# Splitting the weight tiles of an encoder trunk in pairs instead of one by one

## The chip, the cores and the metric

One Trainium2 chip, one NeuronCore. The metric is the time of one execution in device microseconds (us); the median of the runs is compared. Engines: TensorE (PE) multiplies, VectorE (DVE) and ScalarE (ACT) work elementwise, GpSimd (POOL) helps, SyncE (SP) issues the DMAs.

## The reference

A two-layer encoder trunk over 256 tokens of width 2048, float32. Cut to the matrix products that carry the weights:

```python
def reference(x, mem, ...):
    mem_n = rmsnorm(mem, mem_norm_g)
    h = x
    for layer in range(2):
        xn = rmsnorm(h, tok_norm_g[layer])
        if layer == 0:   # gated DeltaNet, two directions, 12 heads of 128, chunks of 64
            mix, q_mem = deltanet_mixer(xn, dn_w_in[0], dn_conv_w[0], ...)
        else:            # gMLP: gelu(u) * (w_s @ rmsnorm(gelu(v)) + b_s), chunks of 128 tokens
            mix, q_mem = spatial_gating_mixer(xn, gm_w_in[0], gm_v_norm_g[0], gm_w_s[0], gm_b_s[0])
        mo = memory_attention(q_mem, mem_n, mem_w_kv[layer])      # 4 heads, 256 memory tokens
        h = h + jnp.concatenate([mix, mo], axis=-1) @ tok_w_out[layer]
        hn = rmsnorm(h, ffn_norm_g[layer])
        h = h + jnp.square(jax.nn.relu(hn @ ffn_w1[layer])) @ ffn_w2[layer]   # hidden 8192
    return rmsnorm(h, final_norm_g)
```

## The kernel before, in words

All weights (some 400 MB) are read once, in tiles of 128 rows by 512 columns, 256 KB. A block is 16 such tiles, that is one strip of 512 columns over 2048 rows; two neighbouring tiles are a slab, so a block has 8 slabs. There are 96 blocks, 1536 tiles. A product in float32 is made from three products with rounded operands: every tile is split into `w_hi`, its rounded value, and `w_lo`, the rest, and the activations (`xT_hi`, `xT_lo`, or `hid_hi`, `hid_lo`) likewise.

Four engines pass each tile on:

- SyncE (`load`, L343) transfers tile kt of block B to `raw[:, kt % 8]`. There are 8 slots; a slot is free again when TensorE has used the tile that was in it (`tile_used`).
- ScalarE (`split`, L981) waits until the tile has landed and copies it, rounded, to `w_hi`; it counts up `hi_ready`.
- VectorE (`split`, L1451) waits for that and subtracts: `w_lo = raw - w_hi`. `w_lo` lies on the same bytes as `raw`. It counts up `tiles_split`.
- TensorE waits for `tiles_split` and multiplies. In `slab` (L467) a tile takes 6 matmuls: for each of two groups of 128 tokens hi x hi, hi x lo, lo x hi (L479, L480, L481). In `up_slab` (L485, the first product of the FFN, whose result is wanted transposed) the tile is the stationary operand and takes 8 matmuls: 4 pieces of 128 columns by 2 (L498, L500).

The order of the work is written out by hand. ScalarE and VectorE split two slabs ahead of TensorE: their loops call `split((t + 2) // 8, (t + 2) % 8)` at step t, and the FFN does the same with `head(B)` (slabs 0 and 1 of a block) and `tail(B)` (slabs 2 to 7). Between the splits stand the other pieces of each engine's work, in program order: `beside(stages, steps)` (L322) takes one stage of the side work after each slab. In the DeltaNet part (blocks 3 to 20) such a stage is a piece of the convolution (`convolve`, L1644, L1657), of the normalisation, of the triangular solve by levels (L1741 on), and so on; GpSimd makes the decay operands (L2104, L2107), two masks (L2128, L2130) and a scaling (L2132) there. In the FFN ScalarE drains a block's result (`up_highs`, L1328), VectorE adds and applies relu (`relu_result`, L1900, L1910), GpSimd squares it (`square_hidden`, L2146), and ScalarE and VectorE split it (`hidden`, L1336 and L1927). At the end of a down block VectorE adds the result to `h` (`add_result`, L1922).

An engine works in program order, so an instruction that waits holds all that stands behind it on its engine.

Of the kernel before, what the change touches and what calls it, by code (L numbers as in the profile page):

```python
# [8 lines left out]
F32 = mybir.dt.float32  # L9
F32R = mybir.dt.float32r  # L10
ACT = mybir.ActivationFunctionType
ALU = mybir.AluOpType
# [115 lines left out]
def encoder_trunk(nc, x, mem, mem_columns, consts, mem_norm_g, tok_norm_g, dn_w_in, dn_conv_w, dn_a_log, dn_dt_bias,  # L128
# [5 lines left out]
    def sem(name):  # L134
        if name not in sem_of:
            sem_of[name] = ctx.enter_context(nc.semaphore(name))
        return sem_of[name]
# [4 lines left out]
    with ctx:  # L142
# [126 lines left out]
        hi_ready = sem("hi_ready")  # L269
        tiles_split = sem("tiles_split")  # L270
        tile_used = sem("tile_used")
# [194 lines left out]
        def _(pe):  # L466
            def slab(B, s, R, parity, kt0, act_hi, act_lo, first, last):  # L467

                for k in range(2):
                    kt = kt0 + k  # L470
                    slot = (2 * s + k) % SLOTS
                    pe.wait_ge(tiles_split, B * 16 + (2 * s + k + 1))
                    start = first and k == 0
# [11 lines left out]
            def up_slab(B, s, R, parity, j, odd=None):  # L485

                for k in range(2):
                    kt = 2 * s + k
                    slot = kt % SLOTS
                    pe.wait_ge(tiles_split, B * 16 + (kt + 1))  # L490
                    for f in range(4):
# [374 lines left out]
            def ffn(layer, next_steps, next_fill=None):  # L866


                for half in range(2):
# [15 lines left out]
                    def last_down(early=3):  # L885
# [5 lines left out]
                        for m in range(2):  # L891
                            tokens = slice(m * P, (m + 1) * P)
                            acc = banks[2 * ((R_FFN[layer] + 11) % 2) + m][:]
                            for kt in range(KT - 2 * early, KT):
                                if m == 0:
                                    pe.wait_ge(tiles_split, B * 16 + kt + 1)
                                slot, ht = kt % SLOTS, KT + kt
# [82 lines left out]
        def _(act):  # L980
            def split(B, s):  # L981

                for kt in (2 * s, 2 * s + 1):
                    slot = kt % SLOTS
                    act.wait_ge(landed[slot], B * 32 + 16 * (kt // SLOTS + 1))
                    act.activation(w_hi[:, slot], raw[:, slot], ACT.Copy).then_inc(hi_ready, 1)  # L986

# [455 lines left out]
        def _(dve):  # L1443
# [7 lines left out]
            def split(B, s):  # L1451

                for kt in (2 * s, 2 * s + 1):
                    slot = kt % SLOTS
                    dve.wait_ge(hi_ready, B * 16 + (kt + 1))
                    dve.tensor_tensor(w_lo[:, slot], raw[:, slot], w_hi[:, slot].bitcast(F32), ALU.subtract  # L1456
                                      ).then_inc(tiles_split, 1)

# [729 lines left out]
```

## Time and profile before

| | us |
|---|---|
| median of 3 runs | 2420.52 |
| lowest and highest run | 2420.32, 2421.28 |
| span of the profiled execution | 2423.1 |
| TensorE, busy in it | 2364.7 |
| VectorE, busy in it | 1557.7 |
| ScalarE, busy in it | 1245.0 |
| GpSimd, busy in it | 169.1 |

The runs agree within 1 us. The span is that of one execution under the profiler, from its first to its last instruction; the page gives no other time of that execution. Busy time of an engine is the time in which at least one of its instructions runs. Matmuls overlap: one of 512 columns is shown as some 390 ns long, but they start 227 ns apart, so a busy TensorE is not one at its peak. The profile names a group by its line in the kernel, its engine, and what it writes and reads; idle time "before" a group is put down to what ended it.

### The profile page before, as it was taken

To read this page: it belongs to the slowest core of one execution; us is meant where nothing else is said; L and a number is where in the kernel's file an instruction comes from. 1 tells how busy PE (TensorE), PEld (TensorE's weight loads), DVE (VectorE), ACT (ScalarE), POOL (GpSimd) and SP (SyncE) were. 2 spreads that over 40 slices of the span, in tenths; PEclk is the share of its full clock that TensorE was granted. 3 is DMA by queue.
4 is the path that set the end of the run, shared out by engine and by line. 5 is a ranking of instruction groups with operands and counts; after the bars stand their busy time and mean duration, and the time that the engine had idled before them with its cause. 6 is when DMAs were issued, how large, how long until landed. Compare 5 with 4: busy or idle time off the path is not lost.

```text
span 2423.1 us, 37472 instructions
## 1 busy us (share of the span) xinstructions
PE 2364.7 (98%) x12069; PEld 2002.1 (83%) x12069; DVE 1557.7 (64%) x2481; ACT 1245.0 (51%) x2205; POOL 169.1 (7%) x123
## 2 busy tenths in 40 slices
PE   8999998998999999999999999999999999999998
PEld 6887886886778888888888888888888888888886
DVE  5567867858767676556765564655767655676654
ACT  5555635635535555444554455554555444555544
POOL 0010102102100100000110000000101000010000
PEclk9999999998999999999999999999999999999999
DMA  6565344343136666666666667566666556666655
GB/s 229 163 172 170 107 123 139 113 134 129 60 108 182 189 189 193 193 192 187 185 186 194 193 183 214 145 184 197 189 190 189 192 194 194 185 186 184 194 193 172
DMA packets 230431, 418.88 MB, mean 173 GB/s; under 512 B 27276, under 2 KB 31261, under 8 KB 230173
## 3 DMA queue, kind: packets, MB, share of 16 engines
q1 hardware_dynamic: 230301, 417.14, 57.0%
q8 instruction: 83, 1.36, 0.2%
q14 instruction: 47, 0.39, 0.0%
HBM read 414.94 MB, written 2.10 MB: 172 GB/s over the span
## 4 chain that ended last, share of the span: by engine, by line
PE 89%; issue 4%; DVE 3%; POOL 1%; DMA 1%; ACT 1%; SPq 0%; DVEq 0%; POOLq 0%; ACTq 0%
PE pair L479 17%; PE pair L481 17%; PE pair L480 17%; PE pair L498 10%; PE aux L498 10%; PE aux L500 5%; PE pair L500 5%; PE aux L669 4%; PE aux L527 3%; DVE w_lo L1456 1%; DVE r L1657 1%; POOL state_out L2107 0%; PE aux L708 0%; DMA raw<-in_tok_w_out 0%; POOL Y L2104 0%
## 5 line engine op out<-in xcount | busy, mean ns | idle before, releaser
L1456 DVE TENSOR_TENSOR w_lo<-raw,w_hi 128x512 fp32r<-128x512 f32 x1536 | 1093.3, 737 | 611.4 <-ACT w_hi L986 607.5
L986 ACT ACTIVATE w_hi<-raw 128x512 fp32r<-128x512 f32 x1536 | 939.0, 633 | 779.1 <-DMA raw<-in_ffn_w 622.2
L479 PE MATMUL pair<-w_hi,xT 128*128 128x512 f32 x960 | 392.2, 409 | 17.7 <-DVE w_lo L1456 8.5
L479 PE MATMUL pair<-w_hi,hid_hi 128*128 128x512 f32 x1012 | 394.3, 390 | 0.0
L481 PE MATMUL pair<-w_hi,hid_lo 128*128 128x512 f32 x1012 | 393.8, 389 | 0.0
L480 PE MATMUL pair<-w_lo,hid_hi 128*128 128x512 f32 x1012 | 393.7, 389 | 0.0
L481 PE MATMUL pair<-w_hi,xT 128*128 128x512 f32 x960 | 379.4, 395 | 0.0
L480 PE MATMUL pair<-w_lo,xT 128*128 128x512 f32 x960 | 378.8, 395 | 0.0
L498 PE MATMUL pair<-xT,w_hi 128*128 128x512 f32 x1024 | 361.0, 396 | 0.4 <-DVE h L1922 0.2
L498 PE MATMUL aux<-xT,w_hi 128*128 128x512 f32 x1024 | 359.1, 395 | 0.0
L500 PE MATMUL aux<-xT,w_lo 128*128 128x256 f32 x1024 | 287.2, 280 | 0.0
L500 PE MATMUL pair<-xT,w_lo 128*128 128x256 f32 x1024 | 286.9, 280 | 0.0
L479 PEld LDWEIGHTS pair<-w_hi,xT 128*128 128x128 f32 x960 | 183.7, 191 | 59.1 <-issue 11.4
L498 PEld LDWEIGHTS pair<-xT,w_hi 128*128 128x128 f32 x1024 | 192.0, 188 | 47.2 <-DVE h L1922 2.2
L498 PEld LDWEIGHTS aux<-xT,w_hi 128*128 128x128 f32 x1024 | 192.0, 187 | 45.0
L481 PEld LDWEIGHTS pair<-w_hi,hid_lo 128*128 128x128 f32 x1012 | 190.0, 188 | 39.5
L479 PEld LDWEIGHTS pair<-w_hi,hid_hi 128*128 128x128 f32 x1012 | 190.0, 188 | 39.4
L480 PEld LDWEIGHTS pair<-w_lo,hid_hi 128*128 128x128 f32 x1012 | 190.0, 188 | 39.1
L481 PEld LDWEIGHTS pair<-w_hi,xT 128*128 128x128 f32 x960 | 183.0, 191 | 40.2
L480 PEld LDWEIGHTS pair<-w_lo,xT 128*128 128x128 f32 x960 | 184.0, 192 | 36.0 <-issue 0.7
L500 PEld LDWEIGHTS aux<-xT,w_lo 128*128 128x128 f32 x1024 | 193.5, 189 | 0.0
L500 PEld LDWEIGHTS pair<-xT,w_lo 128*128 128x128 f32 x1024 | 193.4, 189 | 0.1
(236 smaller groups left out, 1627.1 us busy)
## 6 DMA issues: line engine op xcount, KB each, us to landing
raw<-in_ffn_w SPq DMA_DIRECT2D x1024, 256.0 KB, 3.1
raw<-in_dn_w_in SPq DMA_DIRECT2D x208, 256.0 KB, 2.8
raw<-in_tok_w_out SPq DMA_DIRECT2D x128, 256.0 KB, 3.1
raw<-in_gm_w_in SPq DMA_DIRECT2D x112, 256.0 KB, 2.9
raw<-in_mem_w_kv SPq DMA_DIRECT2D x64, 256.0 KB, 2.8
h<-in_x SPq DMA_DIRECT2D x4, 1024.0 KB, 7.3
r<-in_mem SPq DMA_DIRECT2D x2, 1024.0 KB, 7.4
h<-in_mem_columns SPq DMA_DIRECT2D x2, 1024.0 KB, 6.2
```

Source lines behind the costliest of these rows:

```text
L479: pe.matmul(acc, act_hi[:, kt, tokens], w_hi[:, slot], start=start, stop=False)
L480: pe.matmul(acc, act_hi[:, kt, tokens], w_lo[:, slot], start=False, stop=False)
L481: mm = pe.matmul(acc, act_lo[:, kt, tokens], w_hi[:, slot], start=False, stop=last and k == 1)
L498: pe.matmul(acc[:], w_hi[:, slot, cols], xT[:, kt], start=kt == 0, stop=False, skip_group_check=True)
L500: mm = pe.matmul(acc[:, 0:SEQ], w_lo[:, slot, cols], xT_hi[:, kt, :], start=False, stop=kt == KT - 1, skip_group_check=True)
L527: t = pe.transpose(aux[n % 4][0:src.shape[1], col:col + w], src, cst[0:w, C_ID:C_ID + w])
L669: mm = pe.matmul(bank(n)[part, i * width:(i + 1) * width], lhs(i), rhs(i), start=True, stop=True)
L986: act.activation(w_hi[:, slot], raw[:, slot], ACT.Copy).then_inc(hi_ready, 1)
L1456: dve.tensor_tensor(w_lo[:, slot], raw[:, slot], w_hi[:, slot].bitcast(F32), ALU.subtract).then_inc(tiles_split, 1)
L1657: dve.scalar_tensor_tensor(out=conv[X][:, c], in0=xpad[X][:, c, tap:tap + SEQ], scalar=w, in1=conv[X][:, c], op0=ALU.mult, op1=ALU.add).th ...
```

## The change

ScalarE rounds the two tiles of a slab in one instruction of 128x1024, after it has waited for both to land. VectorE subtracts the two in one instruction. The semaphores count slabs, not tiles: `hi_ready` goes up by 8 in a block instead of 16, and `tiles_split` becomes `pairs_split`. TensorE waits once for a slab, before its first tile. DMAs, slots, matmuls and the order of everything else stay as they are.

```diff
@@ tensor
             def slab(B, s, R, parity, kt0, act_hi, act_lo, first, last):
+                pe.wait_ge(pairs_split, B * 8 + (s + 1))
                 for k in range(2):
                     kt = kt0 + k
                     slot = (2 * s + k) % SLOTS
-                    pe.wait_ge(tiles_split, B * 16 + (2 * s + k + 1))
...
             def up_slab(B, s, R, parity, j, odd=None):
+                pe.wait_ge(pairs_split, B * 8 + (s + 1))
                 for k in range(2):
                     kt = 2 * s + k
                     slot = kt % SLOTS
-                    pe.wait_ge(tiles_split, B * 16 + (kt + 1))
...
                             for kt in range(KT - 2 * early, KT):
-                                if m == 0:
-                                    pe.wait_ge(tiles_split, B * 16 + kt + 1)
+                                if m == 0 and kt % 2 == 0:
+                                    pe.wait_ge(pairs_split, B * 8 + kt // 2 + 1)
@@ scalar
             def split(B, s):
-                for kt in (2 * s, 2 * s + 1):
-                    slot = kt % SLOTS
-                    act.wait_ge(landed[slot], B * 32 + 16 * (kt // SLOTS + 1))
-                    act.activation(w_hi[:, slot], raw[:, slot], ACT.Copy).then_inc(hi_ready, 1)
+                slot = 2 * s % SLOTS
+                for k in range(2):
+                    act.wait_ge(landed[slot + k], B * 32 + 16 * (2 * s // SLOTS + 1))
+                act.activation(w_hi[:, slot:slot + 2], raw[:, slot:slot + 2], ACT.Copy).then_inc(hi_ready, 1)
@@ vector
             def split(B, s):
-                for kt in (2 * s, 2 * s + 1):
-                    slot = kt % SLOTS
-                    dve.wait_ge(hi_ready, B * 16 + (kt + 1))
-                    dve.tensor_tensor(w_lo[:, slot], raw[:, slot], w_hi[:, slot].bitcast(F32), ALU.subtract
-                                      ).then_inc(tiles_split, 1)
+                pair = slice(2 * s % SLOTS, 2 * s % SLOTS + 2)
+                dve.wait_ge(hi_ready, B * 8 + (s + 1))
+                dve.tensor_tensor(w_lo[:, pair], raw[:, pair], w_hi[:, pair].bitcast(F32), ALU.subtract
+                                  ).then_inc(pairs_split, 1)
```

## Rows read from the trace of the kernel before

**Rows 1.** Page, part 1: busy us, share of the span, instructions.

```profile
PE 2364.7 (98%) x12069; PEld 2002.1 (83%) x12069; DVE 1557.7 (64%) x2481; ACT 1245.0 (51%) x2205; POOL 169.1 (7%) x123
```

**Rows 2.** Windows of an FFN up and a down stage: stretch, length, busy, clock.

```profile
777.00:799.00 22.00, 22.00 (x129) 19.42 (x128) 15.65 (x23) 11.64 (x22) 2.27 (x1) 1.00 0.67 190
...
1330.00:1351.00 21.00, 21.00 (x95) 17.38 (x94) 11.01 (x16) 9.76 (x17) 0.00 (x0) 1.00 0.61 192
```

**Rows 3.** List of waits: waiter, releaser, us in total, times, longest.

```profile
PE pair L479 <- DVE w_lo L1456: 8.5, 7, 2.4
...
PE aux L527 <- ACT r L1138: 7.0, 4, 2.5
```

**Rows 4.** Groups by line and shape: count, busy us, mean ns, idle before.

```profile
L986 ACT ACTIVATE w_hi<-raw 128x512 fp32r<-128x512 f32 x1536 | 939.0, 633 | 779.1 <-DMA raw<-in_ffn_w 622.2
...
L1336 ACT ACTIVATE hid_hi<-relu 128x1024 f32 x24 | 25.1, 1045 | 0.0
...
L1456 DVE TENSOR_TENSOR w_lo<-raw,w_hi 128x512 fp32r<-128x512 f32 x1536 | 1093.3, 737 | 611.4 <-ACT w_hi L986 607.5 <-issue 1.4
...
L1927 DVE TENSOR_TENSOR hid_lo<-relu,hid_hi 128x1024 f32 x24 | 29.4, 1226 | 9.4 <-ACT hid_hi L1336 9.4
```

**Rows 5.** Timeline, VectorE, first DeltaNet opening: start, us, idle before, releaser.

```profile
210.10 1.29 DVE L1456 TENSOR_TENSOR w_lo<-raw,w_hi 128x512 fp32r<-128x512 f32 x2 [0.44 <-ACT w_hi L986]
...
233.70 0.69 DVE L1456 TENSOR_TENSOR w_lo<-raw,w_hi 128x512 fp32r<-128x512 f32 x1 [0.31 <-ACT w_hi L986]
```

**Rows 6.** Page, part 6: DMA issues, KB each, median us to landing.

```profile
raw<-in_ffn_w SPq DMA_DIRECT2D x1024, 256.0 KB, 3.1
```

**Rows 7.** Timeline at the start of one FFN up block, four engines.

```profile
799.12 1.69 ACT L986 ACTIVATE w_hi<-raw 128x512 fp32r<-128x512 f32 x3
...
801.12 2.99 DVE L1456 TENSOR_TENSOR w_lo<-raw,w_hi 128x512 fp32r<-128x512 f32 x2
...
801.29 2.27 POOL L2146 TENSOR_TENSOR relu<-relu 128x1024 f32<-128x1024 f32 x1 [19.98 <-DVE relu L1910]
...
803.39 0.39 PE L498 MATMUL aux<-xT,w_hi 128*128 128x512 f32 x1
```

**Rows 8.** Timeline, ScalarE and TensorE, first tiles of the program.

```profile
12.71 2.18 ACT L986 ACTIVATE w_hi<-raw 128x512 fp32r<-128x512 f32 x4
...
14.52 0.76 PE L479 MATMUL pair<-w_hi,xT 128*128 128x512 f32 x1 [2.58 <-issue]
```

**Rows 9.** Timeline, VectorE and TensorE, at the DeltaNet gates.

```profile
103.12 1.29 DVE L1456 TENSOR_TENSOR w_lo<-raw,w_hi 128x512 fp32r<-128x512 f32 x2 [2.52 <-ACT w_hi L986]
...
105.72 0.47 PE L617 MATMUL aux<-gall,cst 128*128 128x12 f32 x3 [1.52 <-DVE gall L1594]
```

**Rows 10.** Timeline, ScalarE and TensorE, behind the second DeltaNet group.

```profile
550.20 1.16 ACT L986 ACTIVATE w_hi<-raw 128x512 fp32r<-128x512 f32 x2 [1.69 <-DMA raw<-in_tok_w_out]
...
552.36 1.94 PE L527 MATMUL aux<-cst,mix 128*128 128x128 f32 x8 [4.40 <-ACT memKT L1030]
```

**Rows 11.** Timeline, ScalarE and TensorE, first block of the gMLP layer.

```profile
1462.84 0.63 ACT L986 ACTIVATE w_hi<-raw 128x512 fp32r<-128x512 f32 x1 [5.62 <-DMA raw<-in_gm_w_in]
...
1463.52 0.63 ACT L986 ACTIVATE w_hi<-raw 128x512 fp32r<-128x512 f32 x1
...
1463.81 0.39 PE L481 MATMUL pair<-w_hi,xT 128*128 128x512 f32 x1
...
1464.30 0.47 PE L479 MATMUL pair<-w_hi,xT 128*128 128x512 f32 x1
```

**Rows 12.** Timeline, VectorE and TensorE, VectorE beside GpSimd.

```profile
254.77 5.52 DVE L1456 TENSOR_TENSOR w_lo<-raw,w_hi 128x512 fp32r<-128x512 f32 x4
...
263.73 0.50 PE L479 MATMUL pair<-w_hi,xT 128*128 128x512 f32 x1 [1.08 <-DVE w_lo L1456]
```

**Rows 13.** Windows around two long TensorE waits; the number before DMA is PEclk.

```profile
403.00:407.00 4.00, 2.94 (x11) 2.75 (x12) 4.00 (x9) 4.00 (x7) 0.00 (x0) 0.60 0.17 57
...
642.00:646.00 4.00, 2.18 (x21) 1.99 (x20) 1.09 (x2) 3.24 (x4) 0.00 (x0) 1.00 0.00 0
```

More of the change, by code:

```diff
@@ L269, in encoder_trunk @@
         hi_ready = sem("hi_ready")
-        tiles_split = sem("tiles_split")
+        pairs_split = sem("pairs_split")
         tile_used = sem("tile_used")
```

## The prediction

> **What bounds the kernel now.** I read the page first, then the groups by line and shape, the list of waits, the windows, and last the timeline at the few places where TensorE stands still.
>
> The busy times show one full engine: TensorE 2364.7 us of a span of 2423.1, VectorE 64% [rows 1]. So both engines whose instructions are merged have spare time over the run, and their saved time is worth nothing where TensorE is full. The windows say where that is: in an up stage and in a down stage of the FFN TensorE is busy 22.00 of 22 us and 21.00 of 21 [rows 2]. 129 matmuls at 8 a tile and 95 at 6 a tile make about 1.35 to 1.4 us a tile; I use 1.36 (a window also counts matmuls that its edges cut). The list of TensorE's waits is short: 8.5 us in seven waits for VectorE's `w_lo`, 7.0 us in four waits for ScalarE's silu, whose input is VectorE's convolution [rows 3]. Nearly all of it is in the DeltaNet part (190 to 700 us).
>
> **What one pair costs.** One tile costs ScalarE 633 ns and VectorE 737 ns (mean). Instructions twice as wide, of the same engines and between SBUF tiles, stand in the trace: 1045 ns and 1226 ns [rows 4]. I take these. Over 768 pairs ScalarE is busy (2 x 633 - 1045) x 768 = 170 us less and VectorE (2 x 737 - 1226) x 768 = 190 us less. But busy times overlap: one tile subtraction alone takes 0.69 us and two back to back 1.29 from first start to last end [rows 5], so where VectorE is really full a pair gains 1.29 - 1.23 = 0.06 us. What it costs is latency. TensorE got the first tile after 0.69 us of VectorE, now after 1.23: 0.53 us later. VectorE began after 0.63 us of ScalarE, now after 1.05: 0.42 later. And ScalarE now waits for the second tile's DMA. TensorE's own gain, half its waits on tiles, I price at nothing: its matmuls follow without a gap where tiles are ready [rows 2].
>
> **Is there room for it in the steady state?** In a down stage a slot is refilled when its tile is used and must be ready 7 tiles later, 9.5 us. Transfer 3.1 [rows 6], ScalarE 0.63, VectorE 0.69: 4.4 us, about 5 spare. In pairs: second slot freed 1.36 later, 3.1, 1.05, 1.23 = 6.7 us, about 2.8 spare. No stall.
> The tightest place is the start of an up block [rows 7]. ScalarE has the tiles from 799.12 on, VectorE comes from the previous block's relu at 801.12, and GpSimd's square (801.29, 2.27 us) gets in between two subtractions: two tiles take until 804.11, TensorE wants the first at 803.39 and the second at 804.75. In pairs: 801.12 + 1.23 = 802.35, 1.0 us early. GpSimd then works for what was left after the first tile, 801.29 + 2.27 - (801.12 + 0.69) = 1.75 us, to 804.10; before, the tile behind it ended 0.55 us later, a pair should need 0.53 more: 805.2, and TensorE wants it at 806.1. It holds, with 0.9 us in hand. Behind a pair that waits for its second transfer stand, on VectorE, the relu, the hidden split and the residual adds; they come later by up to 1.36 + 0.42 us, but the banks they free are wanted a block later, so I price that at nothing. It would cost if TensorE went on in the same bank. So all the FFN blocks stay as they are.
>
> **The places where the pair shows.** Each moves everything behind it.
> - Start: four tiles have landed; VectorE starts when ScalarE's first instruction is done (12.71 + 0.63), TensorE at 14.52 [rows 8]. VectorE is held by its operand work until about then, so 0.53 from its own instruction; those matmuls run at half clock anyway. +0.5.
> - Gates: VectorE waits for a `w_hi` and the reciprocal behind it releases TensorE [rows 9]. 0.42 for ScalarE less 0.06. +0.35.
> - DeltaNet openings, three of them: VectorE is full there; at one place in each it waits for ScalarE [rows 5] (+0.42), and gains 0.06 on each of four pairs. +0.2 each, +0.6. The 0.53 us at the tile waits themselves vanish in the longer waits for silu that follow.
> - The end of the second group: ScalarE waits for a transfer, then frees the bank that TensorE needs [rows 10]; the pair ends there 551.8 instead of 551.36. +0.4.
> - First block of the gMLP layer at 1464.30: the weights arrive just then. ScalarE takes the first tile at 1462.84 and the second, as it lands, at 1463.52; TensorE was idle 1464.30 - 1463.81 - 0.23 = 0.26 us [rows 11]. In pairs: 1463.52 + 1.05 + 0.03 + 1.23 + 0.05 = 1465.9. +1.6, and TensorE is full behind it, so all of it stays.
> - Places of this kind that I have not priced singly: +0.5.
>
> Together +3.9 us. Against it stands one relief. In each DeltaNet group four subtractions alternate with GpSimd's multiplications and take 5.52 us, and TensorE then waits 1.08 us for `w_lo` [rows 12] (three such places, the third shorter). Two pairs meet two GpSimd instructions instead of four: about 3.5 us. But GpSimd ends 1 us later and gets into the masks behind, and TensorE's pair is 0.53 later. The bounds are 0 and 1.1 us at each; I take 0.4, so -1.2.
> The Trainium skill, SBUF — State Buffer, section "Who interferes with whom", says that the lock lasts for a whole instruction and the later one fully blocks; by it the delay of GpSimd behind a pair is up to 1.23 us instead of 0.69, and the relief could be nothing, sum +3.9. The trace shows the blocking: 5.52 us for four tiles that take 2.5 alone [rows 5, 12].
>
> Sum: 3.9 - 1.2 = +2.7. The profiled execution's span is 2423.1 us, 2.6 above the median of the runs, 2420.52, and the page has no other time of its own; I add the change to the median: 2423.2. A measurement of this kernel tells about 0.2% (4.8 us) from no change; this is 0.11%.
>
> **Rivals.**
> 1. Faster: VectorE and ScalarE pace the DeltaNet openings and their saving comes through. For it: the 8.5 + 7.0 us of waits [rows 3]. Price: about ten pairs in each of three openings at 0.06 = 1.8; the relief at its upper bound 3 x 1.1 = 3.3; and shorter waits may keep TensorE's clock. After the 2.5 us wait for silu at 404 the granted clock is 0.60 of 2.4 GHz over 4 us, which is 1.2 GHz for most of it and costs 1.6 us, while a wait of about 1.8 us at 642 to 646 leaves it at 1.00 [rows 13]. Three spells saved: 4.8. With 2.5 us of the losses: 2420.5 - 7.4 = 2413. Against it: 0.06 is all that back-to-back instructions show.
>  By the Trainium skill, VectorE: DVE Perf Modes, section "The TRN2 errata — SBUF-src ops pay a fixed extra latency per instruction", one large instruction pays the fixed cost once; by that rule this change should be faster. The trace agrees on the durations [rows 4]: 1045 ns against 2 x 633, 1226 against 2 x 737.
> 2. Slower, by TensorE's clock: the same losses, no relief, and two of the lengthened waits (1464 grows to 1.8 us, those in the openings by 0.5) pass the point, between about 1.8 and 2.5 us, from which the trace shows the lower clock [rows 13]. 3.9 + 2 x 1.6 = +7.1: 2427.6.
> 3. Slower, by GpSimd's square: it starts 0.17 us after the subtraction [rows 7]. If it comes first it runs to 801.29 + 1.75 = 803.0, the pair is ready at 804.1 and TensorE waits 0.7 us, at each of the 32 up blocks (8192 / 512 columns in two layers): +23 and the above, 2446. It decides if ScalarE's pair is not done at 801.12; it should be done at 800.2.
> 4. The pair costs as much as two instructions (no fixed part saved) and the waits alone count: inside my forecast, no case of its own.
>
> **Numbers.** Forecast (2417 to 2425) 0.63, all of it within 0.2%. Faster, rival 1: 0.11. Slower: rival 2 0.20, rival 3 0.06. The range leaves out rival 3 and about half of rival 1's side: 2415.5 to 2430.
>
> **What would show it.** Right: `w_hi` x768 near 1045 ns and `w_lo` x768 near 1230 ns; a TensorE wait of 1.5 to 1.9 us at the first gMLP block; windows of the FFN as full as before; the DeltaNet stretch within 3 us of its old length. Wrong: a TensorE wait in every up block (rival 3), more or fewer stretches of granted clock under 1 (rivals 1 and 2), or a pair near 1.5 us.

## The result, and the profile after

| | before | with pairs |
|---|---|---|
| median, 16 runs each | 2421.16 us | 2429.70 us |
| lowest to highest | 2419.23 to 2424.95 | 2425.30 to 2437.53 |
| ratio (95% interval) | | 1.0032 (1.0024 to 1.0041) |
| span of the profiled execution | 2423.1 | 2434.1 |
| granted clock of TensorE, mean of the runs | 0.9943 | 0.9926 |

The change costs 8.5 us, 0.32%. I had forecast +2.7 and "within 0.2%". The range, to 2430.0, holds the median by 0.3 us, which is luck: 9 of the 16 runs lie in it, and the loss is three times the forecast one. The clock of before is the mean of 72 runs of it, those measured beside the experiments. Both profiled executions are among the slower ones of their kernel, and differ by more (11.0 us) than the medians do.

Page of the kernel after, part 1, and its groups of the two split instructions (out<-in xcount | busy, mean ns | idle before), against [rows 1, 4]:

```profile
PE 2367.8 (97%) x12069; PEld 2000.5 (82%) x12069; DVE 1463.0 (60%) x1713; ACT 1120.8 (46%) x1437; POOL 200.5 (8%) x123
...
L1455 DVE TENSOR_TENSOR w_lo<-raw,w_hi 128x1024 fp32r<-128x1024 f32 x768 | 993.4, 1299 | 788.4 <-ACT w_hi L986 781.3
L986 ACT ACTIVATE w_hi<-raw 128x1024 fp32r<-128x1024 f32 x768 | 811.6, 1061 | 931.0 <-DMA raw<-in_ffn_w 735.1
```

VectorE is busy 95 us less, ScalarE 124 us less, GpSimd 31 us more, and TensorE, which bounds the kernel, does the same matmuls later. Its waits in the kernel after (us in total, times, longest):

```profile
PE pair L479 <- DVE w_lo L1455: 11.8, 9, 3.0
PE aux L527 <- ACT r L1138: 8.3, 4, 2.5
PE pair L479 <- issue: 6.3, 3, 3.2
...
PE aux L527 <- DVE mix L1823: 2.8, 1, 2.8
PE aux L617 <- DVE gall L1593: 1.9, 1, 1.9
```

The wait for `w_lo` has grown from 8.5 to 11.8 us [rows 3], that for `mix` from 2.2 to 2.8, and that for silu from 7.0 to 8.3. What holds `mix` and silu is seen further up, on VectorE. Its waits for GpSimd's `rs` (the power -1/2 of the sums of squares `ss`) between 90 and 740 us, before:

```profile
DVE tok L1673 <- POOL rs L2123: 3.7, 4, 0.9
...
DVE state_out L1818 <- POOL rs L2135: 0.9, 1, 0.9
```

and after:

```profile
DVE tok L1672 <- POOL rs L2122: 6.9, 6, 1.5
...
DVE state_out L1817 <- POOL rs L2134: 1.5, 1, 1.5
```

I had not looked at this wait. Timeline of VectorE in the second DeltaNet group, before:

```profile
389.25 1.29 DVE L1456 TENSOR_TENSOR w_lo<-raw,w_hi 128x512 fp32r<-128x512 f32 x2 [0.44 <-ACT w_hi L986]
...
397.72 0.17 DVE L1667 TENSOR_SCALAR ss<-ss 128x8 f32<-128x8 f32 x1
397.82 1.30 DVE L1456 TENSOR_TENSOR w_lo<-raw,w_hi 128x512 fp32r<-128x512 f32 x2
400.05 1.29 DVE L1673 TENSOR_TENSOR tok<-aux,rs 128x512 f32<-128x512 f32 x2 [0.93 <-POOL rs L2123]
```

and after:

```profile
394.57 1.23 DVE L1455 TENSOR_TENSOR w_lo<-raw,w_hi 128x1024 fp32r<-128x1024 f32 x1 [0.94 <-ACT w_hi L986]
...
402.91 0.17 DVE L1666 TENSOR_SCALAR ss<-ss 128x8 f32<-128x8 f32 x1
403.00 1.23 DVE L1455 TENSOR_TENSOR w_lo<-raw,w_hi 128x1024 fp32r<-128x1024 f32 x1
405.77 1.29 DVE L1672 TENSOR_TENSOR tok<-aux,rs 128x512 f32<-128x512 f32 x2 [1.54 <-POOL rs L2122]
```

GpSimd's instruction behind it, before (first line) and after:

```profile
397.97 2.05 POOL L2123 TENSOR_TENSOR rs<-ss,neg_half 128x8 f32<-128x8 f32 x1 [8.94 <-DVE ss L1667]
```

```profile
403.15 2.58 POOL L2122 TENSOR_TENSOR rs<-ss,neg_half 128x8 f32<-128x8 f32 x1 [13.37 <-DVE ss L1666]
```

VectorE finishes `ss` and goes on to the next slab; GpSimd, released by `ss`, starts 0.15 us behind that subtraction. Behind one tile it takes 2.05 us, behind a pair 2.58. VectorE then waits 1.54 us where it waited 0.93, and its convolution, ScalarE's silu and TensorE stand behind that. In the same stretch VectorE's wait for `w_hi` is 0.94 in place of 0.44. There are nine `rs` in the run, three in each group, and all nine take 2.54 to 2.64 us, where before all nine took 2.01 to 2.05.

Two things muddy the comparison of single traces. First, TensorE's clock: within blocks 3 to 20 it is at half (1.2 GHz) in several stretches of 3.4 us or a multiple, 34.1 us in all in the trace of before, 30.7 in that of after, though the runs' mean goes the other way. Second, the up stages of the FFN. There are four, one for each half of the hidden columns in each layer. Windows of 20 us in three of them (length, busy with count for PE, PEld, DVE, ACT, POOL, clock, DMA share, GB/s), before:

```profile
780.00:800.00 20.00, 20.00 (x117) 17.62 (x117) 13.58 (x21) 10.39 (x19) 1.30 (x1) 1.00 0.67 192
1110.00:1130.00 20.00, 20.00 (x115) 17.35 (x114) 13.44 (x19) 9.69 (x19) 1.94 (x1) 1.00 0.63 185
1735.00:1755.00 20.00, 20.00 (x117) 17.65 (x116) 13.85 (x22) 10.56 (x19) 0.99 (x1) 1.00 0.65 189
```

and the third of them after:

```profile
1740.00:1760.00 20.00, 20.00 (x115) 17.34 (x115) 12.64 (x13) 8.79 (x12) 2.10 (x1) 1.00 0.67 186
```

TensorE is full and at full clock in all four, and yet does 117 matmuls in one and 115 in another. By the starts in the trace, the long and the short matmul of L498 and L500 follow each other at 230 and 117 ns throughout (1.387 us a tile), or at 241, 120, 236, 113, 233, 117 ns and again (1.413 us a tile). Each stage of these two traces keeps its pattern from its second block to its end. A block of 16 tiles costs 0.42 us more in the slower one, a stage of 8 blocks 3.4 us. Of the 11.0 us between the two traces, 3.4 are of this kind.

### The profile page after: what moved, and what is told of

It is laid out like the page before. It is cut to its first block, busy times and chain, and to the rows that moved or that the text cites. A ratio compares the mean times of both kernels' runs of the same rounds, so it can differ in the third digit from the quotient of the medians.

```text
span 2434.1 us, 36160 instructions
## 1 busy us (share of the span) xinstructions
PE 2367.8 (97%) x12069; PEld 2000.5 (82%) x12069; DVE 1463.0 (60%) x1713; ACT 1120.8 (46%) x1437; POOL 200.5 (8%) x123
## 3 DMA queue, kind: packets, MB, share of 16 engines
q8 instruction: 83, 1.36, 0.2%
## 4 chain that ended last, share of the span: by engine, by line
PE 88%; issue 5%; DVE 3%; POOL 2%; DMA 1%; ACT 1%; SPq 0%; DVEq 0%; POOLq 0%; ACTq 0%
PE pair L479 17%; PE pair L481 17%; PE pair L480 17%; PE pair L498 10%; PE aux L498 10%; PE aux L500 5%; PE pair L500 5%; PE aux L669 4%; PE aux L527 3%; DVE w_lo L1455 1%; DVE r L1656 1%; POOL state_out L2106 0%; POOL Y L2103 0%; PE aux L708 0%; DMA raw<-in_tok_w_out 0%
## 5 line engine op out<-in xcount | busy, mean ns | idle before, releaser
L1455 DVE TENSOR_TENSOR w_lo<-raw,w_hi 128x1024 fp32r<-128x1024 f32 x768 | 993.4, 1299 | 788.4 <-ACT w_hi L986 781.3
L986 ACT ACTIVATE w_hi<-raw 128x1024 fp32r<-128x1024 f32 x768 | 811.6, 1061 | 931.0 <-DMA raw<-in_ffn_w 735.1
L479 PE MATMUL pair<-w_hi,xT 128*128 128x512 f32 x960 | 391.6, 408 | 23.8 <-DVE w_lo L1455 11.8
L498 PE MATMUL pair<-xT,w_hi 128*128 128x512 f32 x1024 | 362.6, 398 | 0.5 <-DVE h L1921 0.3
L498 PE MATMUL aux<-xT,w_hi 128*128 128x512 f32 x1024 | 360.8, 397 | 0.0
L500 PE MATMUL aux<-xT,w_lo 128*128 128x256 f32 x1024 | 287.4, 281 | 0.0
L500 PE MATMUL pair<-xT,w_lo 128*128 128x256 f32 x1024 | 287.2, 281 | 0.0
L498 PEld LDWEIGHTS pair<-xT,w_hi 128*128 128x128 f32 x1024 | 192.2, 188 | 48.6 <-DVE h L1921 2.3
L498 PEld LDWEIGHTS aux<-xT,w_hi 128*128 128x128 f32 x1024 | 192.2, 188 | 46.5
L500 PEld LDWEIGHTS pair<-xT,w_lo 128*128 128x128 f32 x1024 | 193.5, 189 | 0.1
L500 PEld LDWEIGHTS aux<-xT,w_lo 128*128 128x128 f32 x1024 | 193.5, 189 | 0.0
```

Source lines behind the costliest of these rows:

```text
L479: pe.matmul(acc, act_hi[:, kt, tokens], w_hi[:, slot], start=start, stop=False)
L498: pe.matmul(acc[:], w_hi[:, slot, cols], xT[:, kt], start=kt == 0, stop=False, skip_group_check=True)
L500: mm = pe.matmul(acc[:, 0:SEQ], w_lo[:, slot, cols], xT_hi[:, kt, :], start=False, stop=kt == KT - 1, skip_group_check=True)
L986: act.activation(w_hi[:, slot:slot + 2], raw[:, slot:slot + 2], ACT.Copy).then_inc(hi_ready, 1)
L1455: dve.tensor_tensor(w_lo[:, pair], raw[:, pair], w_hi[:, pair].bitcast(F32), ALU.subtract).then_inc(pairs_split, 1)
```

## Experiments

Ratios are against the kernel before on the same chip. Numbers 1 to 4 ran on one chip, 5 to 8 on a second, 9 to 11 on a third and 12 on a fourth, so across these groups ratios are compared and not times. "Theory L" (latency) says that the time is lost where TensorE waits, "theory P" (pattern) that it is lost in slower up stages. Diffs are cut, and against before; where a kernel mixes pairs and single tiles, a pair counts its semaphores up by 2 and TensorE waits per tile.

### 1. TensorE's wait alone

```diff
 def slab / up_slab:
+    pe.wait_ge(tiles_split, B * 16 + (2 * s + 2))
     for k in range(2):
-        pe.wait_ge(tiles_split, B * 16 + (2 * s + k + 1))
```

The wait in the last down block is changed in the same way.

> The kernel before with one edit: TensorE waits once for a slab, for its second tile. ScalarE and VectorE still work tile by tile. Theory L (latency): time is lost only where TensorE stands waiting for w_lo; there it now gets its first tile one subtraction (0.64 us) later. The trace of before has about nine such waits that no longer wait covers (14.5, 209.1, 219.4, 263.7, 388.3, 398.6, 442.8, 588.5, 1464), so at most 9 x 0.64 = 5.8 us, and about 3 us, since in some of them the second tile was late too: 2424. Theory P (pattern): the kernel with pairs lost its time mainly because TensorE runs the up stages in one of two patterns, 1.387 or 1.413 us a tile, and got into the slow one in half 0 of layer 1 (3.4 us over 8 blocks); by it the waits here cost under 2 us and the time moves by more only if the profile shows another stage at 1.413.

2450.26 us, ratio 1.0112 (1.0096 to 1.0129): +27 us, and neither theory had it. Waits of TensorE between 740 and 2300 us, where before has one of 0.2 us:

```profile
PE aux L498 <- DVE w_lo L1456: 9.1, 16, 0.7
PE pair L498 <- DVE w_lo L1456: 5.6, 12, 0.5
PE pair L479 <- DVE w_lo L1456: 3.3, 4, 0.8
```

32 waits, 18.0 us, one for each FFN block whose first slabs follow a relu. VectorE and GpSimd at one of them:

```profile
801.88 2.98 DVE L1456 TENSOR_TENSOR w_lo<-raw,w_hi 128x512 fp32r<-128x512 f32 x2
...
802.04 2.27 POOL L2146 TENSOR_TENSOR relu<-relu 128x1024 f32<-128x1024 f32 x1 [21.10 <-DVE relu L1910]
...
804.92 0.50 PE L498 MATMUL aux<-xT,w_hi 128*128 128x512 f32 x1 [0.51 <-DVE w_lo L1456]
```

It is the place of rows 7: GpSimd's square gets in between the two subtractions, so the slab's second tile is ready only at 804.86, and TensorE now wants it for the first. Before, TensorE worked on the first tile in that time. From start to start of the matmuls around each wait, the longer first one behind it included, the 32 places cost 26.6 us over the usual spacing. That is nearly the whole of the 27 us. Behind a wait the pattern can change: of the seven blocks behind such a wait in half 0 of layer 0, six run at 1.413, where before all ran at 1.387. In the DeltaNet part the merged wait costs nothing: blocks 3 to 20 take 637.4 us in this trace and 640.0 in that of before. In the change itself the wait in the FFN does not happen, because the pair is one instruction that is already running when the square starts (805.76 and 805.92 in its trace). So two of the change's three parts go together: pairs on VectorE are what makes one wait for TensorE affordable.

### 2. ScalarE alone in pairs

```diff
+    act.activation(w_hi[:, slot:slot + 2], raw[:, slot:slot + 2], ACT.Copy).then_inc(hi_ready, 2)
```

> The kernel before with ScalarE alone in pairs (one instruction of 128x1024, counting hi_ready up by 2); VectorE subtracts tile by tile and TensorE waits tile by tile. Theory L: the first subtraction of a slab starts 0.43 us later where VectorE waited for ScalarE. Start +0.4, gates +0.35, block 1 and the openings +0.4 each where ScalarE is the last link, first gMLP block +1.0: together +2.5 to +3.5, so about 2424. ScalarE's 170 us of saved busy time show nothing. Theory P: within 1 us of before, unless the profile shows half 0 of layer 1 at 1.413 us a tile, then +3.4 in that stage.

2432.87 us, 1.0047 (1.0032 to 1.0061), which is +7.8 to +14.8 us and more than theory L's +2.5 to +3.5. ScalarE alone in pairs costs at least what both engines together cost. Its trace (the fastest of its six runs) has `rs` at 2.04 and VectorE's wait for it at 0.93, as before, but its wait for `w_hi` at 0.87; blocks 3 to 20 are 644.1 us long with 34.1 us at half clock. So `rs` can't be the whole of the loss.

### 3. VectorE alone in pairs

```diff
+    dve.wait_ge(hi_ready, B * 16 + (2 * s + 2))
+    dve.tensor_tensor(w_lo[:, pair], raw[:, pair], w_hi[:, pair].bitcast(F32), ALU.subtract
+                      ).then_inc(tiles_split, 2)
```

> The kernel before with VectorE alone in pairs (it waits for both roundings and counts tiles_split up by 2); ScalarE rounds tile by tile, TensorE's waits are written per tile but end per pair. Theory L: the first tile is ready one half of a pair (0.65 us) and one rounding (0.63 us, where VectorE waited for ScalarE) later. Start +0.6 to 1.1, first gMLP block 1463.52 + 0.63 + 0.03 + 1.23 + 0.05 = 1465.5 against 1464.3, +1.2, the waits of the openings +0.6 each: together +4 to +6, 2426. It should be the largest part of the +8.5 us that both together cost. Theory P: under 2 us, and again 3.4 more only with a stage at 1.413 in the profile.

2431.30 us, 1.0032 (1.0021 to 1.0043); L's 2426 is too low by 5. This engine alone costs what both cost, too: the parts don't add up. Its trace shows that VectorE's pair is what holds `rs` (first line), and that the order of the two decides: where `rs` starts first, by 0.03 us, it takes 1.64 us:

```profile
221.59 2.65 POOL L2122 TENSOR_TENSOR rs<-ss,neg_half 128x8 f32<-128x8 f32 x1 [9.47 <-DVE ss L1666]
232.50 1.64 POOL L2122 TENSOR_TENSOR rs<-ss,neg_half 128x8 f32<-128x8 f32 x1 [8.27 <-DVE ss L1666]
...
232.53 2.39 DVE L1455 TENSOR_TENSOR w_lo<-raw,w_hi 128x1024 fp32r<-128x1024 f32 x2
```

VectorE is not held in that order: its first pair there, 0.03 us behind `rs`, takes 1.26 us, against 1.23 elsewhere. All four up stages were at 1.413 in this trace, which is 6.8 us more than in that of before.

### 4. Pairs in the FFN alone

```diff
+FFN_PAIRS, OTHER_PAIRS = True, False
```

> Pairs on ScalarE and VectorE in the FFN's head and tail (blocks 21 to 52 and 64 to 95, about two thirds of all pairs); everywhere else tile by tile. TensorE's waits are written per tile. Theory L: the FFN has no wait that a pair lengthens, so the time stays at that of before, 2421 within 1 us, although ScalarE and VectorE save about 110 and 120 us of busy time. Theory P: if the pairs themselves put TensorE into the slow pattern, half 0 of layer 1 shows 1.413 us a tile and the time is 3.4 us higher, 2424.5; the total of the up stages tells it, whatever the rest does.

2425.30 us, 1.0003 (0.9991 to 1.0016). Theory L holds for the FFN: two thirds of the pairs cost nothing that shows, and gain nothing. The up stages were as in the trace of before, 1.387, 1.413, 1.387, 1.413.

### 5 and 6. Pairs in the DeltaNet part alone; at the start and in the gMLP part alone

```diff
+if not ffn and (not isinstance(B, int) or 3 <= B < 21):     # 5
+if not ffn and isinstance(B, int) and not 3 <= B < 21:      # 6
```

> Pairs on ScalarE and VectorE only in the DeltaNet part (blocks 3 to 20), tile by tile elsewhere, TensorE waits per tile. Pairs in the FFN alone cost nothing that could be measured (ratio 1.0003), so the +8.5 us of the change lie outside it. Theory L (latency, as forecast): in this part +0.35 at the gates and +0.2 to +1.1 at six or seven other waits, less the relief at GpSimd: +3 to +5 us, and nothing elsewhere. Rival C (clock): the part costs what its spells of half clock cost; the traces have 7, 4, 6, 7, 5 of them (before, TensorE waits alone, ScalarE, VectorE, FFN only), so with pairs here about 7 against about 5: +3.4, and the time from block 3 to block 21 should follow their total length, not the number of waits. Theory P: within 1.5 us of before, what is more is up stages at 1.413.

> Pairs on ScalarE and VectorE only in blocks 0 to 2, in the gMLP and output blocks 53 to 63, and in the block or two that lead into each FFN; tile by tile elsewhere. Theory L: start +0.5, block 1 (a new wait at 45.4 in the kernel with pairs) +0.8 to 1.4, first gMLP block +1.6: +3 to +3.5 in all, with a wait of TensorE of about 1.9 us at 1466. Rival P: this part also holds the entry into half 0 of layer 1; if that comes out at 1.413, +3.4 more, 2428.

Number 5: 2432.16 us, 1.0036 (1.0023 to 1.0050), over both L's and C's +3 to +5. Number 6: 2428.00 us, 1.0019 (1.0008 to 1.0030), which is L's +3 to +3.5 within its interval. So the cost lies outside the FFN, and more of it in the DeltaNet part. The shares are rough: the two add up to 0.55%, where the change costs 0.32 to 0.34%. Here the traces are wanted together; a length is from TensorE's first matmul of block 3 to its first of block 21, the half clock is the sum of the stretches in it, and the last column the us a tile in the four up stages:

| kernel | pairs in blocks 3 to 20 | length | at half clock | up stages |
|---|---|---|---|---|
| before | no | 640.0 | 34.1 | 1.387 1.413 1.387 1.413 |
| 4 | no | 637.1 | 23.9 | 1.387 1.413 1.387 1.413 |
| 6 | no | 635.0 | 17.1 | 1.387 1.413 1.413 1.387 |
| 7 | no | 640.8 | 30.7 | 1.403 in all |
| 5 | yes | 641.9 | 27.3 | 1.387 1.413 1.387 1.413 |
| the change | yes | 642.9 | 30.7 | 1.387 1.413 1.413 1.413 |
| 11, the change again | yes | 644.1 | 34.1 | 1.387 1.413 1.387 1.413 |
| 8 | yes | 647.1 | 37.5 | 1.387 1.387 1.387 1.413 |
| 9 | yes, but for 9 slabs on VectorE | 639.8 | 23.9 | 1.387 1.413 1.387 1.413 |
| 10 | yes, but for the openings | 637.9 | 27.3 | 1.387 1.413 1.413 1.413 |

The four without pairs lie within 1.5 us of 630 + 0.31 x (us at half clock), a line drawn through them; experiments 1 and 12, without pairs too, lie 0.1 and 0.8 us under it. The four with pairs lie above it by 3.4, 3.4, 3.5 and 5.5 us (experiments 2 and 3, one engine in pairs, by 3.5 and 2.5): this is latency. A count that needs no line agrees. TensorE's waits in blocks 3 to 20, added up, are 36.0 to 38.1 us in the six traces without pairs and 40.1 to 40.7 us in the four with them.

The four with pairs also have on average 32.4 us at half clock against 26.5, another 5.9 x 0.31 = 1.8 us: this is rival C's part. These means alone would not show it, since the traces without pairs go from 17.1 to 34.1; the granted clock of the runs does (below).

### 7. Four long matmuls, then four short ones, in an up stage

```diff
-for f in range(4):  long(f); short(f)
+for f in range(4):  long(f)
+for f in range(4):  short(f)
```

> The kernel before, tiles singly; in an up stage TensorE does the four 512-column matmuls of a tile first and the four 256-column ones after them, instead of in turn. Same matmuls, same banks, same waits. Theory P says that the step between 1.387 and 1.413 us a tile comes from how these short and long matmuls follow each other, with no wait in it (10 ns more on one matmul in six). If so, another order gives another time a tile: all four stages alike, without the two patterns, and a run-to-run spread under 4 us instead of 12. 1.36 (as in the down stage) would be 32 x 0.4 to 0.85 = 20 us less, 2401; 1.413 everywhere 2427; a load of weights that a short matmul no longer covers could make it slower, 1.5 and 2460. The rival (the pattern is a matter of memory traffic at that moment) expects no change of the two values: 1.387 and 1.413 again, 2421.

2425.27 us, 1.0008 (0.9999 to 1.0018); ten runs within 5.1 us. All four stages run at 1.403 and there are no two patterns. So the step between 1.387 and 1.413 comes with the order in which the matmuls follow each other. The rival, memory traffic at that moment, expected the two values to stay. The hoped for 1.36 did not come; nothing is gained.

### 8. Pairs on both, TensorE's wait per tile

> Pairs on both engines everywhere, as in the change, but TensorE keeps its wait before each tile (the second is always satisfied). All theories: the same time as the change, 2429.7 within 2 us; TensorE's merged wait neither costs nor saves once VectorE works in pairs. If it is more than 3 us above, the 768 removed waits were worth something and my pricing them at nothing was wrong. It is also a second trace of the changed schedule: theory L expects the same lengthened waits (45, 108, 198, 389, 1471) at the same sizes within 0.2 us; theory P expects the up stages to be drawn anew, in particular half 0 of layer 1.

2434.42 us, 1.0050 (1.0037 to 1.0064). That is 4.7 us above the change's 2429.7, over the 3 us that I had set as a sign that 768 waits fewer are worth something. But it is 11.2 us above its own before, where the change is 8.5 and, measured again (number 11), 9.4 above its own, and the intervals overlap (1.0024 to 1.0041, 1.0021 to 1.0048): such a gain is neither shown nor ruled out. The schedule's waits are near those of the change (1.00 for `w_hi`, `rs` at 2.55 to 2.71); half 1 of layer 0 was drawn at 1.387 this time.

### 9. Nine slabs subtracted singly, those behind a sum of squares

```diff
+if not alone:   # alone: this slab is the next one after ss
+    (the pair, as in 3)
```

> Pairs on both engines everywhere (TensorE waits per tile), but nine slabs are subtracted tile by tile: those that VectorE splits right after a sum of squares ss, while GpSimd raises ss to the power -1/2 (rs). In all traces with VectorE in pairs that one GpSimd instruction takes 2.55 to 2.65 us in place of 2.04 and VectorE then waits 1.54 us for it in place of 0.93; with ScalarE alone in pairs it stays at 2.04 and 0.93. Theory S (rs stands behind the pair and is on the chain): rs is 2.04 again at all nine places, the waits 0.93, and about 0.6 us comes back at each of the six to eight that are on TensorE's chain: 3.5 to 5 us less than with pairs everywhere, 2426, blocks 3 to 21 about 640 us. Rival W (VectorE's wait for w_hi, 0.44 grown to 1.0, and the clock carry the cost): rs is 2.04 again, but what comes back there is lost in TensorE's other waits; within 1.5 us of the pairs everywhere.

2433.59 us, 1.0035 (1.0021 to 1.0050), against 2433.26 for the change beside it (number 11): in the time theory S is not confirmed. In the trace its mechanism is. VectorE's waits between 90 and 740 us:

```profile
DVE w_lo L1459 <- ACT w_hi L986: 109.8, 58, 7.4
DVE tok L1683 <- POOL rs L2134: 3.7, 4, 0.9
...
DVE state_out L1829 <- POOL rs L2146: 0.9, 1, 0.9
```

`rs` is back at 2.01 to 2.11 us and the waits for it are those of before, though GpSimd's instruction differs in nothing but what VectorE has running beside it. The length is 2.4 us above the line of the pairless kernels, where the change is at +3.4 and +3.5, so about 1 us of them came back, and six runs that scatter by 9 us can't show that. TensorE's waits in blocks 3 to 20 say the same: 39.3 us, against 40.1 to 40.7. VectorE's wait for `w_hi` (84.3 us before, 109.8 here) stays; rival W is nearer for the larger part, though no run separates that wait.

The traces show one more thing that pairs lengthen, and that these nine slabs don't touch. In the second DeltaNet group the first eight steps of VectorE's convolution fall beside GpSimd's decay operands (L2104, L2107 in before), and TensorE waits for the tile behind them. Before, and then the kernel with pairs:

```profile
379.14 4.09 DVE L1657 SCALAR_TENSOR_TENSOR r<-r,conv_w 128x256 f32<-128x256 f32 x8 [2.65 <-ACT r L1159]
388.26 0.50 PE L479 MATMUL pair<-w_hi,xT 128*128 128x512 f32 x1 [1.35 <-DVE w_lo L1456]
```

```profile
381.64 6.55 DVE L1656 SCALAR_TENSOR_TENSOR r<-r,conv_w 128x256 f32<-128x256 f32 x8 [0.54 <-ACT r L1159]
389.39 0.50 PE L479 MATMUL pair<-w_hi,xT 128*128 128x512 f32 x1 [2.98 <-DVE w_lo L1455]
```

From the first step's start to GpSimd's last operand it is 1.43 us in before and 5.08 with pairs. The eight steps take 4.0 to 6.0 us in the six traces without pairs and 6.5 to 7.5 in the four with them (7.2 here), and the wait behind them 1.1 to 2.1 us against 2.9 to 4.0 (3.6 here). This is read from traces; no experiment moves these steps alone. Nor is all of it loss: the trace of experiment 10, below, has 6.4 and 2.9 us here and lies on the line.

### 10. Single tiles wherever a wait had shown

```diff
+ALONE_BLOCKS = (0, 1, 2, 3, 4, 5, 6, 17, 18, 53, 54, 63, 64)
+split(g * 5 + (B_DN1 + (t + 2) // 8), (t + 2) % 8, t < 12)
```

> Pairs where nothing waits, single tiles where the traces showed a wait: blocks 0 to 6, the first 12 slabs of each DeltaNet group (17 and 18 for the third), 53, 54, 63 and 64 on both engines, and the nine slabs after a sum of squares on VectorE. About 85% of the slabs are still pairs, among them the two in each DeltaNet group that alternate with GpSimd's multiplications. If the cost of the change is the sum of these places, the time is that of before or up to 1 us less (relief of 0.3 us at three places): 2422 to 2424, ratio 0.999 to 1.001, with no wait at 45 and 198 and 1.1 us or less at 1464. If pairs cost something everywhere (more half clock, slower up stages), it stays at 1.002 or more.

2426.45 us, 1.0013 (1.0003 to 1.0023). With 639 of VectorE's 768 pairs kept, 6.8 of the 9.4 us that the change cost beside it (number 11) are gone. Blocks 3 to 20 are on the line (-0.6), with 36.9 us of waits, blocks 53 to 63 take 262.8 us as before, and no wait is left at 45, 198 and 1464. VectorE's waits in the DeltaNet part:

```profile
DVE tok L1691 <- POOL rs L2142: 3.7, 4, 0.9
...
DVE state_out L1837 <- POOL rs L2154: 0.9, 1, 0.9
```

What remains (+2.6 us by the medians) is more than I expected. The mean granted clock is 0.9932, against 0.9941 of the runs of before beside it. Three of four up stages were at 1.413 in its trace; whether pairs in the FFN make that likelier is open. In the seven traces with pairs on VectorE in the FFN, 17 of 28 stages were slow; in the five with single subtractions and the old order of matmuls (before, 2, 5, 6, 12), 8 of 20.

### 11. The change again

> The change itself, unaltered, beside the same runs of before as the two above, and for another trace of it. 2430 within 2.5 us, +7 to +9 on before. What must be the same in a second trace is what the schedule sets (rs at 2.6 us, w_lo waiting 1.0 us for w_hi in the openings, TensorE 1.9 us at the first gMLP block); what theory P holds to be drawn anew at each execution may differ: the four up stages at 1.387 or 1.413, and the number of half-clock spells.

2433.26 us, 1.0034 (1.0021 to 1.0048). The waits that the schedule sets are the same (`rs` 2.54 to 2.64, `w_hi` 0.93, 1.54), and half 0 of layer 1 is at 117 matmuls in this trace, 115 in the first one of the same program:

```profile
1740.00:1760.00 20.00, 20.00 (x117) 17.65 (x116) 13.06 (x12) 9.09 (x13) 2.60 (x1) 1.00 0.67 189
```

So two executions of one program can differ in it. All four up stages of this trace are as in that of before, and yet it is 8.6 us longer (2431.7 against 2423.1): theory P, that the change lost its time by the pattern, falls.

### 12. Experiment 1, but per tile in one slab of each up block

```diff
+if s == 2:   # up_slab only
+    pe.wait_ge(tiles_split, B * 16 + (kt + 1))
```

> The kernel of the first experiment (tiles rounded and subtracted singly, TensorE waits once a slab), which took 27 us more than before. Its trace has 31 waits of TensorE for w_lo in the FFN, one at the start of nearly every up block, all before slab 2 of the block: there GpSimd's square gets in between the two subtractions and the second one is shown 2.38 us long. Here TensorE waits before each tile in slab 2 of the up blocks alone, and once a slab everywhere else. Theory Q (the square between the two subtractions is the whole cost, and one instruction for the pair avoids it): the 27 us vanish, 2424 within 2.5 us, no wait of TensorE in the up stages. Rival (fewer, later waits cost something at every slab): over 2430.

2428.61 us, 1.0019 (1.0010 to 1.0028). 22 of the 27 us vanish once one slab in eight has its two waits back; the trace shows none in the up stages. I had forgotten the first block of each down stage, which follows a relu too:

```profile
PE pair L479 <- DVE w_lo L1459: 3.3, 4, 0.8
...
911.20 4.19 DVE L1459 TENSOR_TENSOR w_lo<-raw,w_hi 128x512 fp32r<-128x512 f32 x4
...
911.36 2.28 POOL L2149 TENSOR_TENSOR relu<-relu 128x1024 f32<-128x1024 f32 x1 [19.97 <-DVE relu L1913]
...
914.33 0.47 PE L479 MATMUL pair<-w_hi,hid_hi 128*128 128x512 f32 x1 [0.83 <-DVE w_lo L1459]
```

Four such waits at about 1.0 us between matmuls make 4 of the 4.6 us that are left. The first matmul of the program, which still waits for a slab, comes 0.6 us later behind what precedes it (3.18 us in place of 2.58). Theory Q, that the square between the two subtractions is the cost, holds for the up blocks; its 2424 was missed by these places.

## Where the prediction was right, and where it was wrong

The time came out inside the range; the sum behind it did not. Its term for the DeltaNet openings was too small by far, and the clock, which it left out, took part.

**Durations and the FFN: right.** A pair takes ScalarE 1061 ns (forecast 1045) and VectorE 1225 in the median (1226), 1299 in the mean, since those beside GpSimd take up to 2.9 us. The 170 and 190 us saved were sums of mean durations; what the page counts as busy time of these two groups fell by 127 and 100. The change's traces have no new wait for `w_lo` in the FFN before its last down block (0.4 us there; those of experiments 9 and 10 have one of 1.0 at the first down block), and experiment 4 puts the FFN's cost at 0. Rival 3 did not occur, since ScalarE's pair was done in time (VectorE's pair follows the relu without a wait, at 805.76); experiment 1 shows that its place and its price were real: I had 0.7 us at each of 32 blocks, 23 us, and a wait that meets the same square costs 27.

**The terms at single places: right in size.** Start +0.5: the first matmul went from 14.52 to 15.07, and what it waits behind the work before it from 2.58 to 3.18 us (3.18 to 3.25 in the other traces with pairs on both engines there; when that work ends differs between traces by 0.9 us). Gates +0.35: the wait for `gall` from 1.5 to 1.9. End of the second group +0.4: its two waits (for `memKT` or `mix`, and for `xT`) are 5.6 us in the mean of the four traces with pairs, 5.0 in the four without. First gMLP block +1.6: in the trace after

```profile
1468.46 1.06 ACT L986 ACTIVATE w_hi<-raw 128x1024 fp32r<-128x1024 f32 x1 [4.63 <-DMA raw<-in_gm_w_in]
1469.55 2.56 DVE L1455 TENSOR_TENSOR w_lo<-raw,w_hi 128x1024 fp32r<-128x1024 f32 x2 [4.46 <-ACT w_hi L986]
1470.88 0.47 PE L479 MATMUL pair<-w_hi,xT 128*128 128x512 f32 x1 [1.72 <-issue]
```

and blocks 53 to 63 take 264.6 us (mean of the change, 8 and 11) against 263.0 (before, 4, 5 and 7): +1.6.

**The relief: right at a place, too large in sum.** Two pairs and GpSimd took 3.43 us in place of 5.52 (forecast 3.5), and TensorE's wait there 0.74 in place of 1.08: 0.34 at a place, forecast 0.4. But only two places have such a wait (1.06 to 0.75 at the second); before the change TensorE has none at the third. The relief is 0.65 us and not 1.2.

```profile
259.08 3.43 DVE L1455 TENSOR_TENSOR w_lo<-raw,w_hi 128x1024 fp32r<-128x1024 f32 x2
...
267.71 0.50 PE L479 MATMUL pair<-w_hi,xT 128*128 128x512 f32 x1 [0.74 <-DVE w_lo L1455]
```

**The DeltaNet openings: wrong.** "+0.2 each, +0.6" is the term that failed. In the three openings TensorE's waits are 0.7, 1.6 and 0.6 us longer with pairs (means of the four traces with and the four without, the wait at 198 left out): 2.8 us stand where I had 0.6.

The one wait that I priced there, for ScalarE, grew by 0.5 where I had said 0.42 (0.44 to 0.94). What I did not look for is who stands behind VectorE's longer instruction on another engine: `rs` on GpSimd, nine times, 0.6 us later each, with VectorE itself waiting for it at seven. I had also said that what the tiles lose there vanishes in the waits for silu that follow. In experiment 1 it does: in the first two openings they shrink from 2.47 to 1.88 us. With pairs they stay at 2.47, because silu's own input comes later.

I had even written down the rule, from the Trainium skill, SBUF — State Buffer, section "Who interferes with whom", that the later instruction is fully blocked, and used it only to ask whether the relief could be nothing. Applied to `rs` it gives the loss: the pair of 403.00 ends at 404.23, GpSimd's 1.64 us (experiment 3) after that end at 405.87; shown is 403.15 + 2.58 = 405.73. The trace agrees. It does not in the other order: `rs` first, VectorE's pair 0.03 us later is not held for the 1.64 us (experiment 3). The rule speaks against the change at this place and for it at the relief.

In the first opening `rs` is the whole of the loss by the traces: the waits there are 4.2 us before, 4.8 to 4.9 with pairs, and 4.2 again in experiment 9. In the second it is not. There the wait behind the convolution beside GpSimd's decay operands is 1.8 us longer in the mean (3.4 against 1.6), and those just before it together 0.5 shorter. Experiment 9 leaves that wait as it is, and gave back only about 1 us. How much of the rest is this and how much the longer wait for `w_hi` stays open. In all, blocks 3 to 20 took 3.4 us more than the line where I had +0.35 + 0.6 + 0.4 - 1.2 = +0.15.

**The unpriced places: too low.** "+0.5" should have been about 2.5. In block 1 VectorE's sum of squares stands behind a pair and starts at 40.28 in place of 38.66; GpSimd's `rstd`, ScalarE's drain and TensorE (1.19 us; 0.6 and 0.5 in the traces of 8 and 11) wait behind it. At 198 ScalarE had waited 5.0 us for a slab whose transfers stand near one of 1 MB (3.4 at that place before), and TensorE waits 0.9 us for the pair. In the first FFN block of layer 1 (1712) the residual add comes 0.1 to 0.7 us later. The first two on TensorE:

```profile
45.45 0.74 PE L527 MATMUL aux<-cst,Y 128*128 128x128 f32 x5 [1.19 <-ACT Y L1011]
...
197.96 0.49 PE L479 MATMUL pair<-w_hi,xT 128*128 128x512 f32 x1 [0.89 <-DVE w_lo L1455]
```

**The clock: rival 2's mechanism joined in.** I kept it out of the forecast, as a case apart. The mean granted clock of all runs fell from 0.9943 to 0.9926 and, measured again, 0.9922, also in experiments 2, 3, 5, 8 and 9 (0.9918 to 0.9929), and not in 4 and 6 (0.9947, 0.9940): it goes with pairs in the DeltaNet part. By the traces it costs 1.8 us. By the runs' means it is an estimate of 2.6: 0.0017 of the clock are 8.2 us more at half clock, at 0.31 each. Rival 2's 2427.6 was the nearest of my four times, though without the relief that did come.

The place that rival 2 named, the first gMLP block, did fall to the lower level in one of the five traces with pairs on both engines there, that of experiment 9. TensorE's waits before it were 1.90 us in experiment 8 (first line) and 2.00 in experiment 9 (second); the clock is the number before the last two:

```profile
1469.00:1476.00 7.00, 5.10 (x23) 3.89 (x22) 3.11 (x3) 6.38 (x7) 0.00 (x0) 1.00 0.62 189
1466.00:1473.00 7.00, 5.00 (x15) 3.87 (x15) 3.73 (x4) 6.28 (x7) 0.00 (x0) 0.76 0.39 123
```

Behind the second wait eight matmuls start 427 ns apart in place of 227, which is the 1.6 us that I had priced, and blocks 53 to 63 take 266.9 us in place of 264.6. Still, a length of wait "between about 1.8 and 2.5 us" from which the clock falls is not what the traces show. In that of before it falls behind the wait of 1.52 us at the gates [rows 9]:

```profile
105.00:111.00 6.00, 5.28 (x22) 4.57 (x23) 3.82 (x11) 2.37 (x5) 0.00 (x0) 0.72 0.18 51
```

Together: start 0.5, blocks 0 to 2 0.8 (75.9 us against 75.1), blocks 3 to 20 3.4 and the clock 1.8, gMLP 1.6, block 64 about 0.5: 8.6 us, against 8.5 measured at first and 9.4 when measured again. The parts come from single traces, so that they add up so well is partly chance. **TensorE's own gain** of half its waits I priced at nothing, and experiment 8 doesn't show one.

No version here beats the kernel before. Pairs in the FFN alone (experiment 4) equal it, within -0.1 and +0.2%.

## What to carry to other kernels

Merging two instructions on an engine that isn't the bound saves busy time that nobody needs, and delays the first half for everyone who waits: go through those behind it on its own engine, those that want its first half, and those on another engine that it keeps out while it runs. Where a neighbour's instruction can slip in between two halves, a consumer's merged wait costs far more than the merged instruction (27 against 8.5 us here), so merge both or neither. When two traces differ by 0.3%, take a second trace of the same program first: here half-clock stretches and the pace of the up stages differ between two traces of the same kernel.

## What the runs showed of the hardware that I had not expected

- Alternating matmuls of 512 and 256 columns have two steady rhythms, 347 and 353.3 ns a pair on average, with no wait in either, at granted clock 1.00. Behind an interruption of TensorE it can be the other one (experiment 1). Four stages of 3.4 us each would be enough for the scatter of the kernel before (72 runs, 2418.1 to 2429.9); that they make it is not shown. Four long and then four short ones have one, 1.403 us a tile. What sets the rhythm stays open.
- GpSimd's instruction on eight columns took 1.64 us where it started before VectorE's subtraction, 2.04 behind one of a single tile, and 2.54 to 2.71 behind one of two. VectorE's pair, started 0.03 us behind it, took 1.26 us, as if nothing stood beside it. Which comes first was decided by 0.02 to 0.17 us.
